# One fused two-layer transformer step on one core: value blocks in row form, row sums ahead of the first weights, the feed-forward norm's scale on the products, the output in four parts

## The reference

```python
mk, mv = split(rms_norm(mem) @ w_mem_kv); av, v_a, v_g = parts of h @ w_in
h2 = rms_norm_2(x, norm2_w)          # x * rsqrt(mean(x*x) + eps) * norm2_w, row by row
x = x + (silu(h2 @ w_ffn_gate) * (h2 @ w_ffn_up)) @ w_ffn_down
return rms_norm_2(x, final_norm_w)
```

## Time and profile before

| | |
|---|---|
| median of 3 runs | 3200.23 us (3197.53 to 3201.62) |
| the profiled execution | 3202.73 us |
| its span, first to last instruction | 3201.0 us |
| PE busy | 3047.4 us, 95% of the span, 19874 matmuls |
| PEld busy | 2641.0 us, 83% |
| DVE busy | 1674.6 us, 52% |
| ACT busy | 1356.6 us, 42% |
| POOL busy | 70.8 us, 2% |
| HBM read | 511.29 MB, 160 GB/s over the span |
| mean granted clock of PE | 0.981 |

### The profile page before, as it was taken

One profiled execution on the slowest core, in us unless ns is written; L12 is line 12 of the kernel. 1 busy time (PEld: TensorE's weight loads), 2 busy tenths in 40 slices (PEclk: granted clock), 3 DMA queues, 4 the chain that ended last, 5 costly groups with the idle time before them and its releaser, 6 DMA issues.

```text
span 3201.0 us, 46147 instructions
## 1 busy us (share of the span) xinstructions
PE 3047.4 (95%) x19874; PEld 2641.0 (83%) x19874; DVE 1674.6 (52%) x1984; ACT 1356.6 (42%) x1552; POOL 70.8 (2%) x186
## 2 busy tenths in 40 slices
PE   5999999889999999999999999999999999999998
PEld 5888888867998887879999879988887888888886
DVE  4555545447555556644455456655555444444444
ACT  4433333434454444444444434444444444444333
POOL 3000000000100000000000000000000000000000
PEclk9999999999999999999999999999999999999999
DMA  5333333335666555555555645566555666666554
GB/s 165 107 106 106 111 113 113 107 96 173 177 195 190 165 152 145 184 184 159 168 170 175 186 133 152 165 186 190 187 194 158 183 185 188 183 182 199 187 190 145
DMA packets 354816, 516.42 MB, mean 161 GB/s; under 512 B 18192, under 2 KB 137124, under 8 KB 353588
## 3 DMA queue, kind: packets, MB, share of 16 engines
q1 hardware_dynamic: 353844, 510.27, 53.2%
q0 software_dynamic: 768, 3.20, 0.4%
HBM read 511.29 MB, written 2.11 MB: 160 GB/s over the span
## 4 chain that ended last, share of the span: by engine, by line
PE 91%; DVE 4%; ACT 4%; issue 1%; DMA 0%; SPq 0%; ACTq 0%; DVEq 0%
PE gp L1325 18%; PE gp L1326 18%; PE gp L1327 18%; PE gp L1334 10%; PE gp L1335 9%; PE gp L1336 9%; PE ps L1479 4%; PE ps L1376 1%; PE ps L1440 1%; PE ps L1465 1%; DVE arena L967 1%; ACT w_hi L544 1%; DVE w_lo L857 1%; PE ps L1426 1%; DVE arena L851 1%
## 5 line engine op out<-in xcount | busy, mean ns | idle before, releaser
L857 DVE TENSOR_TENSOR w_lo<-w_raw,w_hi 128x1024 fp32r<-128x1024 f32 (+2 forms) x976 | 1169.1, 1203 | 976.5 <-ACT w_hi L544 975.2
L544 ACT ACTIVATE w_hi<-w_raw 128x1024 fp32r<-128x1024 f32 (+2 forms) x976 | 1012.3, 1040 | 1266.7 <-PE gp L1327 847.9
L1334 PE MATMUL gp<-h_hi,w_hi 128*128 128x256 f32 x2464 | 728.6, 296 | 7.9 <-DVE w_lo L857 5.3
L1335 PE MATMUL gp<-h_lo,w_hi 128*128 128x256 f32 x2464 | 697.0, 283 | 0.0
L1336 PE MATMUL gp<-h_hi,w_lo 128*128 128x256 f32 x2464 | 696.6, 283 | 0.0
L1325 PE MATMUL gp<-w_hi,h_hi 128*128 128x512 f32 x1728 | 688.6, 399 | 0.8 <-DVE h_lo L911 0.8
L1326 PE MATMUL gp<-w_hi,h_lo 128*128 128x512 f32 x1728 | 682.5, 395 | 0.0
L1327 PE MATMUL gp<-w_lo,h_hi 128*128 128x512 f32 x1728 | 682.3, 395 | 0.0
L1334 PEld LDWEIGHTS gp<-h_hi,w_hi 128*128 128x128 f32 x2464 | 473.3, 192 | 21.6 <-DVE w_lo L857 5.5
L1335 PEld LDWEIGHTS gp<-h_lo,w_hi 128*128 128x128 f32 x2464 | 473.6, 192 | 1.7
L1336 PEld LDWEIGHTS gp<-h_hi,w_lo 128*128 128x128 f32 x2464 | 472.4, 192 | 0.0
(11 more groups left out here) (269 smaller groups left out, 2136.3 us busy)
## 6 DMA issues: line engine op xcount, KB each, us to landing
w_raw<-in_w_in SPq DMA_DIRECT2D x384, 512.0 KB, 3.7
w_raw<-in_w_ffn_gate SPq DMA_DIRECT2D x88, 512.0 KB, 4.0
w_raw<-in_w_ffn_up SPq DMA_DIRECT2D x88, 512.0 KB, 4.3
w_raw<-in_w_ffn_down SPq DMA_DIRECT2D x88, 512.0 KB, 3.6
w_raw<-in_w_in SPq DMA_DIRECT2D x136, 256.0 KB, 3.2
w_raw<-in_w_in SPq DMA_DIRECT2D x128, 192.0 KB, 2.8
w_raw<-in_w_mem_kv SPq DMA_DIRECT2D x32, 512.0 KB, 4.1
w_raw<-in_w_o SPq DMA_DIRECT2D x32, 512.0 KB, 3.9
```

What stands on the lines that cost most here:

```text
L544: act.activation(w_hi[:, slot, 0:size], w_raw[:, slot, 0:size], ACT.Copy).then_inc(sem("hi_done"), 1)
L857: dve.tensor_tensor(w_lo[:, slot, 0:size], w_raw[:, slot, 0:size], w_hi[:, slot, 0:size].bitcast(F32), ALU.subtract)\
L1334: pe.matmul(o, wh, x_hi[k], start=(k == 0 and c % 2 == 0), stop=False, skip_group_check=True)
L1335: pe.matmul(o, wh, x_lo[k], start=False, stop=False, skip_group_check=True)
```

## The change

Four edits.

1. The eight value blocks become row form; the evacuation writes them straight into a tile with tokens on partitions (a_v, c_v, q_v, l_v). The four turns, DVE's copies and the waits on them go. Some tiles move in the arena (c_z, the first memory rows). POOL's wait before the GLA zeros is on another semaphore.
2. At the start, ACT takes a root of a spare column first, then sums x, then rounds the first unit, then takes the root of the sums, then rounds two more; DVE makes its first three w_lo between the first and the second scaled piece. SP issues the lora units ahead of the small row loads.
3. The feed-forward norm: DVE multiplies each finished piece of x by the gain alone (`g_x`), three pieces are turned inside the last "o2" block and the fourth behind the second unit of "ffn"; the inverse root is applied to the products: as the scale of Silu in the gate evacuation and in a scalar_tensor_tensor in the up evacuation, each in two halves of 512 (one per half of the rows).
4. The output is scaled and stored in four parts: 1536 columns and then 512 of each row half; the last 512 columns take gain and inverse root in one DVE instruction.

```diff
-    phase("Q", wide("w_in_2", Q_COL, 6, "h", "q_cols"))
-    phase("L", wide("w_in_2", L_COL, 6, "h", "l_cols"))
+    phase("Q", values(wide("w_in_2", Q_COL, 6, "h", "q_cols"), 4, 5))
+    phase("L", values(wide("w_in_2", L_COL, 6, "h", "l_cols"), 2, 3))
 ...
# ACT, evacuation of the gate block
-                    act.activation(f_t[:, 0, :], g, ACT.Silu).then_inc(done, 1)
+                    act.wait_ge(sem("scale_ready"), 1)
+                    for t in range(2):
+                        ins = act.activation(f_t[:, 0, t * 512:(t + 1) * 512], g[:, t * 512:(t + 1) * 512], ACT.Silu,
+                                             scale=stat[:, 8 + t:9 + t])
 ...
# ACT, start
-            for n in range(LEAD):
-                hi(n)
+            act.wait_ge(sem("ident_ready"), 1)
+            act.activation(small[:, 27:28], small[:, 26:27], ACT.Sqrt)
             for j in range(4):
                 row_sums(j, n_junk, lambda j: act.wait_ge(sem(f"x_landed{j}"), 16))
-            act.wait_ge(sem("ident_ready"), 1)
+            hi(0)
             row_root()
+            hi(1)
+            hi(2)
 ...
# DVE, evacuation of the up block
-                    dve.tensor_tensor(f_t[:, 1, :], f_t[:, 0, :], g, ALU.mult).then_inc(done, 1)
+                    for t in range(2):
+                        part = slice(t * 512, (t + 1) * 512)
+                        ins = dve.scalar_tensor_tensor(f_t[:, 1, part], g[:, part], stat[:, 8 + t:9 + t], f_t[:, 0, part],
+                                                       ALU.mult, ALU.mult)
 ...
# DVE, start: norm(fill, 1, LEAD)
                 scaled(0)
+                for n in range(lead):
+                    lo(n)
                 scaled(1)
 ...
# DVE, o2 blocks: after each block's residual add
+                        if next_rows and m == m1 + 3 and n - first[m] in (2, 4, 6):
+                            j = (n - first[m]) // 2 - 1
+                            cross_low(tiles4(h_lo, j), tiles4(h_hi, j))
+                    if next_rows and m >= m1:
+                        j = m - m1
+                        if j == 0:
+                            seen.need("gain_landed", 16)
+                        wait_evacuated(dve, m)
+                        cols = gain[:, 512 * j:512 * j + 512].unsqueeze(1).to_broadcast([P, 2, 512])
+                        dve.tensor_tensor(g_x[j], piece(xr, j), cols, ALU.mult).then_inc(sem("norm_rows"), 1)
 ...
# PE
+            def turn_next(j):
+                pe.wait_ge(sem("norm_rows"), 8 + j + 1)
+                turn_rows(CROSS["norm2_w_2"] + j, g_x[j])
 ...
-            turn(values(q_vraw))
-            pe.wait_ge(sem("turn_copied"), pe_n["turn"])
             fill = filler(unit, ["L", "down"])
-            attention("q", 8, 1, q_q, q_k, att_v, fill, 6)
+            attention("q", 8, 1, q_q, q_k, q_v, fill, 6)
 ...
             for m in range(m0, m1 + 4):
                 for n in block_units(m):
-                    if n >= first[m0] + 4:
-                        unit(n)
+                    unit(n)
+                    if n == first[m0] + 1:
+                        turn_next(3)
 ...
# DVE and SP, end
-            dve.wait_ge(sem("rows_scaled"), 4)
-            dve.tensor_scalar(xr[:, 0, :], xr[:, 0, :], stat[:, 8:9], None, ALU.mult).then_inc(sem("out_ready0"), 1)
+            dve.wait_ge(sem("rows_scaled"), 3)
+            dve.tensor_scalar(xr[:, 0, 0:1536], xr[:, 0, 0:1536], stat[:, 8:9], None, ALU.mult).then_inc(sem("out_head0"), 1)
+            for a in range(2):
+                dve.scalar_tensor_tensor(xr[:, a, 1536:D], xr[:, a, 1536:D], stat[:, 8 + a:9 + a], gain[:, 1536:D],
+                                         ALU.mult, ALU.mult).then_inc(sem(f"out_tail{a}"), 1)
```

## The result

The changed kernel takes 3159.59 us (median of 4 runs, 3157.99 to 3161.69), the kernel before on the same chip 3200.14 (4 runs, 3197.53 to 3201.62). The ratio is 0.9872, 95% interval 0.9858 to 0.9887: 40.55 us less, where 40.3 were forecast. The profiled execution took 3159.61 us, span 3157.7.

The account below looks back on a forecast made before the run. The prediction took TensorE (PE), holding 91% of the chain that ended last, as the bound. Its terms, 2.0 + 18.3 + 10.8 + 8.9 + 0.3 = 40.3 us, gave 3159.9 us, range 3154 to 3168.

Parts of the forecast that it names:

- Turns: After four value blocks, PE's 16 transposes and waits for DVE's copies fall away: 18.3 us saved.
- Turn "a": First turn removed, at 767.54 to 773.05: 5.28 us bare plus 0.8 of slow clock behind it, together 6.1.
- the first rival: Part of the turns returns as waits on w_lo, 5 us, and 3.4 of clock: 3168; chance 0.08.
- turn "l": Turn ahead of the GLA chain, 1881.19 to 1885.63: 4.2 us saved, not swallowed by the chain's end.
- the bound of 1.7 us either way: Behind the last turn, where a slow stretch falls may change: half of 3.4 us.
- Rows form: Eight value blocks of 8 units, each unit 0.031 us shorter: 2.0 us saved; bounds 0 and 2.5.
- Turn "q": Turn ahead of the first score product, 1586.66 to 1590.14: 3.5 us saved; the wait for ACT's evacuation stays.
- The start: New order on SP, ACT and DVE: second h_hi at 21.2 instead of 32.03, 10.8 us saved; bounds 8.6 and 11.6.
- The norm: Between "o2" and "ffn": 12.1 us today less 3.2 for four turns, 8.9 saved; bounds 7 to 9.5.
- The split evacuations: 11 gate and 11 up evacuations in halves: costed at nothing; PE waits once DVE's two exceed 5.4 us.
- the rival: Split evacuations become the bound in "ffn", needing 9.6 us on DVE: slower than before, 3207; chance 0.02.
- The end: First store issued 0.3 us earlier, 0.3 saved; bounds -1.5, +0.8. By the skill's figures, four serial loads need 12.8 us.

Follow-up runs that it names:

- undo_values: Changed kernel with the value blocks back in column form and their four turns, copies and waits restored: 3180.07 us, +20.5 against 3159.6.
- undo_start: Changed kernel with the former order of the start restored on SP, ACT and DVE: 3169.71 us, +10.1 against 3159.6.
- root_first: Changed kernel with the root ahead of the first rounding on ACT and the second scaling ahead of the low parts on DVE: 3154.96 us, -4.6.
- undo_norm: Changed kernel with the feed-forward norm bare in front of its blocks and the scale on the rows again: 3168.69 us, +9.1.
- pad8: Changed kernel with eight idle DVE reciprocals ahead of the split evacuation of each of 11 up blocks: 3219.95 us, +60.4.
- pad2: Changed kernel with two idle DVE reciprocals ahead of the split evacuation of each of 11 up blocks: 3158.64 us, -1.0.
- undo_out: Changed kernel with two stores of a whole row half and the scaling of 2048 columns restored: 3159.70 us, +0.1.
- act_only: Changed kernel with SP's former order of issues at the start, keeping the new order on ACT and DVE: 3160.76 us, +1.2.
- idle_turns: Changed kernel with 16 idle transposes added at each of the four former turns, without copies or waits: 3165.86 us, +6.3.

## Why the prediction was right

The time, 3159.59 for 3159.9, came from terms that hold for the most part: turns, start and norm, 38.0 of the 40.3 us, came out within 1.2 us each and at their places. That the sum is right to 0.3 is in part luck, since a row form worth less than forecast and slow stretches at places without an edit, which no term holds, go against each other, and the medians of two groups of runs are themselves sure to some 1 to 2 us only.

- **Turns.** Forecast 18.3 = 6.1 + 4.5 + 3.5 + 4.2. By the positions of the units: 5.3, 4.8, 3.2 and 3.8, 17.1. Turn "a" itself gave its 6.1, as the slow stretch behind it went with it: from 753.60 in the trace of before to the end of "gate_b" the distance between the traces grows from 12.95 to 19.03. But 0.8 had been lost at the head of the same stage: the 10.2 us slow stretch that follows PE's wait of 9.7 us there ended with the wait's own work before, and now runs 1.6 us into the products. So the clock's part was sized right at its place, and moved to another. Nothing came back on w_lo in "gate_b" or "gate_c"; PE's waits on it are one, in GLA. That settles the first rival, together with undo_values. In GLA the wait grew from 5.3 to 6.8. The z products start at 1885.63 in the kernel before and at 1852.06 now, and the wait ends 15.3 and 15.4 us later:

```profile
1900.96 0.58 PE L1334 MATMUL gp<-h_hi,w_hi 128*128 128x256 f32 x1 [5.31 <-DVE w_lo L857]
```

```profile
1852.06 1.99 PE L1663 MATMUL ps<-arena 16*128 16x256 f32 x8
...
1867.45 0.58 PE L1370 MATMUL gp<-h_hi,w_hi 128*128 128x256 f32 x1 [6.84 <-DVE w_lo L883]
```

So the chain moved with the turn, as forecast. The slow stretch that stood behind turn "l" (1887.4 to 1890.8) lay ahead of this wait and had cost nothing: without it PE only waits 1.5 longer. So of the bound of 1.7 us either way, the gain could not have come from there. The 0.4 between the 4.2 of this turn and its 3.8 is clock too: behind the end of that wait the granted clock stays at 0.50 for 4.5 us (to 1871.9) where it did for 3.5 (to 1904.5).
- **Rows form.** Forecast 2.0, and this is the term that was mis-sized. What is left for it at most: 43.3 - 11.6 (start) - 17.1 - 8.9 - 0.1 (end) = 5.6. At places that no edit touches, three slow stretches are shorter by 3.4 us each (one in the last pair, one ahead of "Q", one in "V6") and one is longer by as much (in "mem"), a net 6.8 us of slow clock or 3.4 us of time, which leaves 2.2. The pitch is as forecast. In this stretch of "mem" the products start 0.2333 us apart (170 steps from 1108.20 to 1147.87; the 173 take in the two that the edges cut), 2.80 a unit:

```profile
1108.00:1148.00 40.00, 40.00 (x173) 1.00 0.63 186
```

But not all blocks keep the gain. By the first product of each block, counted through both traces, each value block in "mem" and "Q" gains some 0.2 us, 0.9 for the four. A4 and A5 gain 0.2 each and have lost most of it when the next value or A block begins (12.18 ahead of A4, 12.30 behind A5). The two in "L", woven into the attention, lose 0.4 together: the distance is 29.85 ahead of them and 29.46 behind. That is some 0.6 us in all, where 2.0 stood; the bound of 0 had been given for small work between the units. Turn "q", read the same way, gives 3.5, its forecast; the 3.2 above hold the loss in "L". The rest of the 2.2 lies in differences of a few tenths where no edit is (0.4 in the first block of "C"), and what makes them stays open.
- **The start.** Forecast 10.8, with the first transposes at 15.9, and the second h_hi at 21.2. Measured 15.63 and 20.84, 11.2 us; undo_start gives 10.1. The intermediate steps hold too: the first rounding starts at 13.03 and ends before the root at 13.56, where 13.1 and 13.8 were forecast. The landing times were the part with the widest bounds, and the value between two rows was right to 0.1 for the first unit: gain landed at 12.1 and the four lora units at 13.0, 13.9, 14.8 and 15.6, 0.9 apart where 1.05 was forecast. The step with most effect, that three w_lo now stand between scaled(0) and scaled(1), is there: PE's second group of transposes waits 1.26 us for it, and taking it away is part of root_first's 4.6.
- **The norm.** Forecast 8.9; by the positions 34.3 to 43.2, 8.9, by undo_norm 9.1. The cover of 14.8 us for the chain of piece 3 was enough, as PE has no idle there. One step was off without effect: the fourth g_x is done 3.4 us behind the last product of "o2" instead of 2.7, since a w_lo stands ahead of the add on DVE, and PE comes for it after 5.8.
- **The split evacuations.** Costed at nothing with a point of 5.4 us. They take 1.5, pad8 puts the point at 5.3, and the 3.4 of pad2 are covered. But the rival's arithmetic lacked a term: beyond the point, a block costs its idle and 1.6 us of clock. To lose 46.7 us, 4.2 per block, DVE would have needed 5.3 + 2.6 = 7.9 us, not 9.6. Against the 1.5 measured the rival was still far off, but nearer than I wrote. The Trainium skill, "VectorE: DVE Perf Modes", section "The TRN2 errata", gives each instruction that reads SBUF a fixed extra cost: the halves came out at 2 x 0.746 against 1.221, 0.27 dearer than the whole, so the direction agrees with this trace. The instruction changed too, from tensor_tensor to scalar_tensor_tensor, and no run separates that from the halving.
- **The end.** Forecast 0.3, found 0.1 in the traces: from the last product to the end 12.97 us before and 12.84 after. The first store is issued 5.91 us behind the last product instead of 6.18, which is the 0.3, but from the first issue's start to the last one's end SP takes 2.94 us where it took 1.13 (the third issue alone 1.20, where the first two take 0.36 each), and from the first issue to the end are 6.9 us instead of 6.8. The changed kernel's SP timeline:

```profile
3150.77 2.94 SPq L409 DMA_DIRECT2D out_x<-xr  x4
```

Four stores of 2 MB in all are over 6.9 us after the first is issued, and two in undo_out 6.8, so a fixed cost for each store does not show as a sum. The Trainium skill, "DMA: Bandwidth & Descriptors", section "Anatomy of one DMA", has its 2 us of fixed cost for a DMA on the GpSimd path; the prediction left that condition out, and the loads and stores here are issued by SyncE, so its 12.8 us were no measure of them.
- **The profiled execution.** I forecast 3162.4 for it, and it took 3159.61. The 2.8 us are for the most part clock: before its last product the kernel before ran 109.2 us at 0.50 and the changed kernel 92.1, 17.1 less. 13.6 of it stood at stops that the change removes (3.4 behind turn "a", 6.8 at the feed-forward norm, 3.4 behind turn "l"), 3.4 came new at the start, and the net 6.8 above fell away where no edit is: 3.4 us of time that no term holds, and the forecast missed by 2.8. This may be why the profile of before lay 2.5 above its median while this one lies on it; no second profile of either kernel shows it. The theory that most of the gain is clock, and not tied to the parts, falls with the four undone parts, which each give their own share back.

What was noted as a sign under the wrong number: the transposes of "mem" (32) are on line 1455 of the changed kernel, the former 1412; its line 1412 holds the norms' and the merges' turns.

## What to carry to other kernels

Where one engine holds nine tenths of the chain, walk along it from product to product at each place the diff touches, and subtract one pitch: those differences, with the term for the rows form, added up to within 1 us of the gain between the medians and 3 us of that between the two profiles, and undoing the parts one by one gave the same shares within 1 to 2 us. Price every stop of that engine at its idle plus what the clock loses behind it, in forecasts of losses too, but only where no wait follows that takes up the loss, as it did behind turn "l". A gain in pitch counts only where the engine runs undisturbed. Before work is moved forward to fill a wait, look which block's end comes with it: an evacuation that slips ahead of the next hand-over takes the gain back.

## What the runs showed of the hardware that I had not expected

- A stop of PE of 4.0 us between stretches at full clock was followed by 3.4 us at a granted clock of 0.50 each of 11 times (pad8, the first of its stretches above). The 11.4 us recorded at 0.50 at the end of the changed kernel's trace cost nothing, as no product is left there.
- The same place has slow stretches of different length from one profiled execution to the next, without an edit near it: behind the norm ahead of "Q" 10.2 us in the kernel before and in act_only, 6.8 in the changed kernel and in idle_turns; in "mem" 3.4 or 6.8. pad2 and pad8 differ from the changed kernel by idle instructions behind 2440 us alone, and yet have 3.4 in "mem" and 10.2 ahead of "Q", where it has 6.8 and 6.8. A stretch longer by 3.4 us costs 1.7 of time, and two such differences would make up most of the spread between the runs of one kernel (3.7 us); that they do is only argued, as one execution of each kernel was profiled. Differences of 1 to 2 us between two profiles of this kernel say nothing unless the clock of their stretches is laid beside them, as in act_only, whose span is the same as that of the changed kernel (3157.8) though its first units come 2.35 late.
- Four loads of 0.5 MB issued back to back landed at 5.15, 6.82, 8.10 and 9.55 in the changed kernel's trace, one every 1.5 us; ACT's sums of the four pieces start at 5.17, 6.84, 8.26 and 9.69.
